# Feed-forward input on un-normed rows: the first two tiles before the norm is known, the row factor applied at their eviction

## The chip, the core and the metric

One core of one Trainium2 chip runs two transformer-like blocks over 512 tokens of width 1024, in float32. The metric is the time of the whole program on the device, in microseconds (us). The engines of the core that appear below are TensorE (PE: matmuls, with PEld for its weight loads), VectorE (DVE), ScalarE (ACT), GpSimd (POOL) and SyncE (SP, which issues the loads of weights). Each runs its own list of instructions in order and waits for the others by semaphores.

## The reference, cut to what matters

```python
def rms_norm(x, g):
    xf = x.astype(jnp.float32)
    xf = xf * lax.rsqrt(jnp.mean(xf * xf, axis=-1, keepdims=True) + RMS_EPS)
    return (xf * g.astype(jnp.float32)).astype(x.dtype)

def modulate(h, shift, scale):
    return h * (1.0 + scale[:, None, :]) + shift[:, None, :]

def swiglu(h, w_in, w_out):
    gate, up = jnp.split(h @ w_in, 2, axis=-1)
    return (jax.nn.silu(gate) * up) @ w_out
...
        h = modulate(rms_norm(x, norm_g[l, 0]), shift[:, 0], scale[:, 0])
        x = x + 0.5 * gate[:, 0, None, :] * swiglu(h, ffn1_w_in[l], ffn1_w_out[l])
        ... token mixer on a second norm ...
        h = modulate(rms_norm(x, norm_g[l, 2]), shift[:, 2], scale[:, 2])
        x = x + 0.5 * gate[:, 2, None, :] * swiglu(h, ffn2_w_in[l], ffn2_w_out[l])
```

With r the factor of a token's row (one number per token), c the combined scale per channel and s the shift per channel, a tile of the feed-forward input is W^T (x c r + s). That equals r times W^T (x c), plus W^T s, which is one number per output channel.

## The kernel before, in words

All activations lie transposed: channels on the 128 partitions, the 512 tokens along the free axis, so a tensor of width 1024 is 8 slabs of 128x512. Each float32 product is made of three passes on parts of reduced width: weights and activations are each split in a high and a low part, and a slab of 128 channels costs three matmuls of 512 columns (high by high, low by high, high by low; lines 431 to 433). The profile calls the activation parts `act_hi` and `act_lo`, the weight parts `w_hi` and `w_lo`.

Weights arrive in chunks of 128x1024, in four rotating buffers. SP loads a chunk into `w_raw` (L426), ACT copies it to the high part (`split_hi`, L382), DVE subtracts to get the low part (`split_lo`, L390), PE uses it for one tile of output in one of four PSUM banks. The splitting runs two chunks ahead of PE (`AHEAD = 2`); where a stage ends, the last splits in its loop belong to the first two chunks of the next stage. The stages follow one another as a list, and on each engine the order is that in which the code is written.

The change touches the two places where a projection back to the residual is followed by a norm and a feed-forward input. The first is `out1`, norm 1, `ffn1_in` (around 700 us), the second `out2`, norm 3, `ffn2_in` (around 1630 us). Each goes as follows:

- `residual` on DVE: for each of the 8 output tiles, split chunk f+2, wait for tile f, add it to the residual slab f. ACT squares the slab (`square`; twice for norm 1, which folds two norms into one and needs two sums), POOL adds the squares of slabs 1 to 6 up.
- `rms_sum` on PE: the squares of all channels are summed per token by matmuls with one column, 8 instructions for norm 3 and 16 for norm 1 (L809). The profile records two entries for each such instruction of plain float32. Then DVE makes a reciprocal, ACT a square root, DVE a diagonal of the factors (`rms_diagonal`), and PE spreads it over the partitions by matmuls with 128 columns into PSUM (L817, for norm 1 also L821).
- `rms` on DVE and `norm_hi` on ACT: for each slab, DVE multiplies residual, scale and factor (L2024), ACT adds the shift and writes `act_hi` (L1535), DVE subtracts to get `act_lo` (L2024). Semaphore `h_ready` counts the slabs.
- `first_pair` on PE: two tiles of the feed-forward input at once, slab by slab as they come, so that six matmuls follow each slab. Then two more tiles, then ten more rounds of four tiles in a loop. In each round, tile 0 and tile 2 are gates (ACT's `Silu`), tile 1 and tile 3 are multiplied with them by DVE, and the product is split into high and low parts for the next stage.

## Time and profile before

| | |
|---|---|
| median of 3 runs | 2020.28 us (2018.68 to 2022.92) |
| the profiled execution's own time | 2020.2 us |
| its span in the trace | 2018.4 us |
| PE busy | 1944.0 us, 96% of the span |
| DVE, ACT, POOL busy | 1000.2, 789.9, 171.1 us |
| mean granted clock of TensorE | 0.984 of full speed |

The span is the time between the first and the last record; the program's own time is 1.8 us longer. Busy times overlap between engines and don't add up to the span. The clock is the share of full speed that was granted to TensorE; it takes two levels, 1.2 and 2.4 GHz, which show as 0.50 and 1.00, and a stretch that holds both shows something between.

### The profile page before, as it was taken

To read this page: it belongs to the slowest core of one execution; us is meant where nothing else is said; L and a number is where in the kernel's file an instruction comes from. 1 tells how busy PE (TensorE), PEld (TensorE's weight loads), DVE (VectorE), ACT (ScalarE), POOL (GpSimd) and SP (SyncE) were. 2 spreads that over 40 slices of the span, in tenths; PEclk is the share of its full clock that TensorE was granted. 3 is DMA by queue.
4 is the path that set the end of the run, shared out by engine and by line. 5 is a ranking of instruction groups with operands and counts; after the bars stand their busy time and mean duration, and the time that the engine had idled before them with its cause. 6 is when DMAs were issued, how large, how long until landed. Compare 5 with 4: busy or idle time off the path is not lost.

```text
span 2018.4 us, 25631 instructions
## 1 busy us (share of the span) xinstructions
PE 1944.0 (96%) x9438; PEld 1590.2 (79%) x9438; DVE 1000.2 (50%) x1434; ACT 789.9 (39%) x1320; POOL 171.1 (8%) x192
## 2 busy tenths in 40 slices
PE   6999999999999999999999899999899999999998
PEld 5888878766788778888887787899688878888886
DVE  5687866575444353333335668454443353333332
ACT  4334333365432344334224644343423244334232
POOL 1101110000000300000001300044000110000000
PEclk9999999999999999999998999999899999999999
DMA  8957913211133322333323223211234323333331
GB/s 291 310 177 233 309 45 97 73 43 38 33 111 118 100 82 88 101 96 93 107 80 110 67 75 90 57 43 53 63 94 130 115 74 94 94 104 91 98 96 50
DMA packets 330629, 212.85 MB, mean 105 GB/s; under 512 B 21358, under 2 KB 315179, under 8 KB 330031
## 3 DMA queue, kind: packets, MB, share of 16 engines
q1 hardware_dynamic: 319024, 170.58, 29.0%
q0 software_dynamic: 10368, 37.75, 5.3%
q10 hardware_dynamic: 1150, 3.35, 0.5%
q8 instruction: 56, 0.92, 0.2%
q14 instruction: 31, 0.25, 0.0%
HBM read 204.31 MB, written 7.35 MB: 105 GB/s over the span
## 4 chain that ended last, share of the span: by engine, by line
PE 84%; DVE 8%; ACT 3%; DMA 2%; issue 2%; ACTq 1%; POOL 0%; DVEq 0%; SPq 0%; POOLq 0%
PE psum L431 24%; PE psum L433 23%; PE psum L432 23%; DVE delta_qkv_T L2024 2%; PE psum L1324 2%; DMA ada_w<-in_ada_w 1%; DVE ada_sum L2024 1%; PE psum L1111 1%; PE psum L1139 1%; DVE w_lo L390 1%; PE psum L1122 1%; PE psum L1007 1%; PE psum L1023 1%; PE psum L1270 1%; DVE act_lo L2024 1%
## 5 line engine op out<-in xcount | busy, mean ns | idle before, releaser
L431 PE MATMUL psum<-act_hi,w_hi 128*128 128x512 f32 x1616 | 648.5, 401 | 8.7 <-DVE act_lo L2024 5.9
L433 PE MATMUL psum<-act_hi,w_lo 128*128 128x512 f32 x1616 | 631.9, 391 | 0.0
L432 PE MATMUL psum<-act_lo,w_hi 128*128 128x512 f32 x1616 | 631.4, 391 | 0.0
L390 DVE TENSOR_TENSOR w_lo<-w_raw,w_hi 128x1024 fp32r<-128x1024 f32 x306 | 382.4, 1252 | 353.2 <-ACT w_hi L382 327.2
L382 ACT ACTIVATE w_hi<-w_raw 128x1024 fp32r<-128x1024 f32 x306 | 319.9, 1053 | 194.3 <-PE psum L433 183.0
L431 PEld LDWEIGHTS psum<-act_hi,w_hi 128*128 128x128 f32 x1616 | 304.9, 189 | 88.5 <-issue 24.1
L433 PEld LDWEIGHTS psum<-act_hi,w_lo 128*128 128x128 f32 x1616 | 304.5, 188 | 65.0
L432 PEld LDWEIGHTS psum<-act_lo,w_hi 128*128 128x128 f32 x1616 | 305.2, 189 | 61.3 <-issue 1.2
L722 POOL TENSOR_TENSOR squares<-squares 128x512 f32<-128x512 f32 x30 | 46.7, 1564 | 1251.1 <-ACT squares L1511 906.9
L431 PE MATMUL psum<-ffn_hi,w_hi 128*128 128x512 f32 x352 | 139.5, 396 | 0.0
L433 PE MATMUL psum<-ffn_hi,w_lo 128*128 128x512 f32 x352 | 139.0, 395 | 0.0
L432 PE MATMUL psum<-ffn_lo,w_hi 128*128 128x512 f32 x352 | 139.0, 395 | 0.0
L1567 ACT ACTIVATE ffn_hi<-ffn_tmp 128x512 f32 x44 | 27.8, 632 | 210.8 <-DVEq L2469 210.8
L2024 DVE SCALAR_TENSOR_TENSOR residual<-psum,params,residual 128x512 f32<-128x512 f32 x24 | 18.0, 751 | 151.4 <-PE psum L433 151.4
L2024 DVE SCALAR_TENSOR_TENSOR ada_sum<-ada_w,params,ada_sum 128x1024 f32<-128x1024 f32 x63 | 80.8, 1282 | 16.8 <-DMA ada_w<-in_ada_w 14.8
L2021 DVE TENSOR_TENSOR ffn_tmp<-ffn_tmp,psum 128x512 f32<-128x512 f32 x44 | 30.2, 687 | 113.4 <-PE psum L433 113.4
L433 PEld LDWEIGHTS psum<-ffn_hi,w_lo 128*128 128x128 f32 x352 | 66.2, 188 | 15.8
L431 PEld LDWEIGHTS psum<-ffn_hi,w_hi 128*128 128x128 f32 x352 | 66.2, 188 | 15.5
L432 PEld LDWEIGHTS psum<-ffn_lo,w_hi 128*128 128x128 f32 x352 | 66.2, 188 | 15.5
L2024 DVE SCALAR_TENSOR_TENSOR delta_qkv_T<-psum,params,delta_qkv_T 128x511 f32<-128x511 f32 (+3 forms) x96 | 60.3, 647 | 35.8 <-ACT delta_qkv_T L1855 33.7
L2021 DVE TENSOR_TENSOR ffn_lo<-ffn_tmp,ffn_hi 128x512 f32 x44 | 30.5, 693 | 46.8 <-ACT ffn_hi L1567 46.8
L431 PE MATMUL psum<-merged_hi,w_hi 128*128 128x512 f32 x128 | 50.6, 395 | 0.0
(343 smaller groups left out, 2331.7 us busy)
## 6 DMA issues: line engine op xcount, KB each, us to landing
w_raw<-in_ffn_w_in SPq DMA_DIRECT2D x88, 512.0 KB, 3.7
ada_w<-in_ada_w POOLq DMA_DIRECT2D x72, 512.0 KB, 5.7
w_raw<-in_w_in SPq DMA_DIRECT2D x68, 512.0 KB, 3.8
w_raw<-in_mix_w_in SPq DMA_DIRECT2D x52, 512.0 KB, 3.7
w_raw<-in_ffn_w_out SPq DMA_DIRECT2D x32, 512.0 KB, 3.8
w_raw<-in_ffn_w_out SPq DMA_DIRECT2D x16, 384.0 KB, 3.3
w_raw<-in_w_branch_a SPq DMA_DIRECT2D x8, 512.0 KB, 3.7
w_raw<-in_w_out SPq DMA_DIRECT2D x8, 512.0 KB, 3.7
```

The source lines that it names most:

```text
L382: act.activation(WHI[:, n % 4, :], RAW[:, n % 4, :], ACT.Copy).then_inc(w_hi, 1)
L390: dve.tensor_tensor(WLO[:, n % 4, :], RAW[:, n % 4, :], WHI[:, n % 4, :].bitcast(F32), ALU.subtract).then_inc(w_lo, 1)
L431: pe.matmul(out, whi, hhi, start=start, stop=False)
L432: pe.matmul(out, whi, hlo, start=False, stop=False)
L433: return pe.matmul(out, wlo, hhi, start=False, stop=stop)
L722: ins = pool.tensor_tensor(SQ[:, q, :], SQ[:, q, :], SQ[:, square_slot(r, k) + q, :], ALU.add)
L1007: mm = pe.matmul(PS[:, 5 + n % 2, 0:T - j * P], QK1[:, 8 + 2 * h + e, j * P:j * P + P], QK1[:, 2 * h + e, j * P:T], start=(e == 0), stop=( ...
L1023: mm = pe.matmul(PS[:, PV_BANK[t % 2], 0:MD + 1], DP[:, h % 2, o:o + P], VTOK[:, j, h, :], start=(j == 0), stop=(j == i))
L1324: mm = pe.matmul(PS[:, bank, (h % 4) * P:(h % 4) * P + P], left(h), right(h), start=True, stop=True)
L1567: act.activation(dst, src, ACT.Copy).then_inc(u_hi, 1)
L2021: return dve.tensor_tensor(o, a, b, op)
L2024: return dve.scalar_tensor_tensor(o, a, s, b, op0, op1)
```

## The change

For `ffn1_in` and `ffn2_in`, the first two tiles are made from the residual times the channel scale, without factor and shift (`raw_pair`). Their activations are written while the projection back still runs: ACT copies each slab with its scale into `act_hi` in `square`, DVE makes `act_lo` in `raw_lo`, one slab later than the residual add. PE runs the two tiles as soon as the projection is done, with the sums of squares, the sums for the shift and the spreading of the factors put in between the slabs. The shift's part, W^T s, is made by DVE from the raw weights of the two chunks (`bias_part`: a product of 128x1024 and a reduction of 1024 to 128 that reads every 128th element) and by two matmuls of one column. The norm then writes the true `act_hi` and `act_lo` over the raw ones, slab by slab, once PE has used them (`raw_used`), and tiles 2 and 3 take the place of the first pair. At eviction DVE multiplies both raw tiles by the factors, ACT applies `Silu` with the shift's sum as bias, and DVE adds the other sum and multiplies. The first round of the loop is written out for this on DVE and ACT, and the factors are copied from PSUM into SBUF by ACT (`RROW`).

```diff
             def rms_sum(r):
...
-                if r == 4:
-                    return
+
+            def rms_spread(r):
+
                 pe.wait_ge(sem("rms_diagonal"), r)
...
+            def raw_pair(r):
+
+                pl = Place(AHEAD_OF[r], 0)
+                banks = [pe_open(pe, pl, t) for t in range(2)]
+                pe.wait_ge(w_lo, pl.chunk + 2)
+                for kk in range(KD):
+                    pe.wait_ge(h_ready, RAW_AT[r] + kk + 1)
+                    for t, bank in enumerate(banks):
+                        n, a = pl.chunk + t, slice(kk * P, kk * P + P)
+                        mm = mm3(pe, bank, WHI[:, n % 4, a], WLO[:, n % 4, a], HHI[:, kk, :], HLO[:, kk, :],
+                                 kk == 0, kk == KD - 1)
+                        if kk == KD - 1:
+                            mm.then_inc(chunk_done, 1)
+                    if kk < KD - 1:
+                        mm.then_inc(sem("raw_used"), 1)
+                    if kk == 1:
+                        rms_sum(r)
+                    elif kk == 2:
+                        pe.wait_ge(sem("bias_parts"), r)
+                        for t in range(2):
+                            mm = pe.matmul(PS[:, 7, t:t + 1], BSUM[:, t, :], ONES[:, 0:1], start=True, stop=True)
+                        mm.then_inc(sem("bias_sum"), 1)
+                    elif kk == 4:
+                        rms_spread(r)
+
+            def after_norm(r):
+
+                raw_pair(r)
+                name = AHEAD_OF[r]
                 pl = Place(name, 0)
-                first_pair([(pl, 0), (pl, 1)], base)
-                for k in range(2, pl.nb):
-                    pe_tile(pe, pl, k, k, KD, HHI, HLO)
+                first_pair([(pl, 2), (pl, 3)], H_AT[r])
...
                 e.then_inc(sem("squares_ready"), 1)
+                if r in RAW_AT:
+                    act.activation(HHI[:, k, :], XT[:, k, :], ACT.Copy, scale=col(COEF_OF[r] + k)).then_inc(sem("h_hi"), 1)
...
+            def before_norm(r):
+
+                pl = Place(AHEAD_OF[r], 0)
+                split_hi(act, pl, 2)
+                root(r)
+                split_hi(act, pl, 3)
+                norm_hi(r, SHIFT_OF[r])
...
+                        if first and f == 0:
+                            act.wait_ge(sem("raw_scaled"), 1 + (name == "ffn2_in"))
+                            act.activation(FS[:, 0, :], FS[:, 0, :], ACT.Silu, bias=col(AG)).then_inc(sem("rows_then_gate"), 1)
...
-                dve.wait_ge(sem("rms_spread"), r)
+                if r in RAW_AT:
+                    split_lo(dve, Place(AHEAD_OF[r], 0), 2)
+                    split_lo(dve, Place(AHEAD_OF[r], 0), 3)
+                    dve.wait_ge(sem("bias_sum"), r // 2 + 1)
+                    dve.tensor_copy(col(AG, 2), PS[:, 7, 0:2]).then_inc(sem("bias_parts"), 1)
+                if r in RAW_AT:
+                    dve.wait_ge(sem("rows_then_gate"), 2 * (r // 2) + 1)
+                    rows = RROW[:]
...
+            def raw_lo(r, k):
+
+                dve.wait_ge(sem("h_hi"), RAW_AT[r] + k + 1)
+                stt(HLO[:, k, :], XT[:, k, :], col(COEF_OF[r] + k), HHI[:, k, :].bitcast(F32), ALU.mult, ALU.subtract)\
+                    .then_inc(h_ready, 1)
+
+            def bias_part(r, t):
+
+                n = Place(AHEAD_OF[r], 0).chunk + t
+                dve.wait_ge(w_loaded[n % 4], 16 * (n // 4 + 1))
+                chained(tt(BPART[:].rearrange("p (k n) -> p k n", n=P), RAW[:, n % 4, :].rearrange("p (k n) -> p k n", n=P),
+                           b3(col(SHIFT_OF[r], KD), P), ALU.mult))
+                ins = dve.tensor_reduce(BSUM[:, t, :], BPART[:].rearrange("p (k n) -> p n k", n=P), AX, ALU.add)
+                chained(ins) if t == 0 else ins.then_inc(sem("bias_parts"), 1)
+
+            def residual(name, per_tile, gate_col, normed=False, r=None):
 
                 pl = Place(name, 0)
                 for f in range(KD):
+                    if r and f:
+                        raw_lo(r, f - 1)
+                    if r and f in (6, 7):
+                        bias_part(r, f - 6)
...
+                        if first and f == 0:
+                            tiles_ready(dve, pl, 1)
+                            cnt.mark(tt(FS[:, 0, :], RROW[:], PS[:, pl.bank(0), :], ALU.mult))
+                            chained(tt(UTMP[:], RROW[:], PS[:, pl.bank(1), :], ALU.mult))
+                            dve.sem_inc(sem("raw_scaled"), 1)
+                            for t in range(2):
+                                dve.sem_inc(bank_free[pl.bank(t)], 1)
+                            dve.wait_ge(sem("rows_then_gate"), 2 + 2 * (name == "ffn2_in"))
+                            chained(stt(FS[:, 0, :], UTMP[:], col(AG + 1), FS[:, 0, :], ALU.add, ALU.mult))
```

The order of instructions on DVE at the end of `out1`, before the change, from the fifth add to the residual on (`residual<-psum,residual` is the add, `w_lo<-w_raw,w_hi` a split; the last two splits are those of the first two chunks of `ffn1_in`):

```order
L2021 TENSOR_TENSOR residual<-psum,residual 128x512
L390 TENSOR_TENSOR w_lo<-w_raw,w_hi 128x1024
L2021 TENSOR_TENSOR residual<-psum,residual 128x512
L390 TENSOR_TENSOR w_lo<-w_raw,w_hi 128x1024
L2021 TENSOR_TENSOR residual<-psum,residual 128x512
```

The same piece after the change, from the sixth add on (`act_lo<-residual,...` is `raw_lo`, `bias_parts` and `bias_sums` are `bias_part`; what each waits for stands behind it):

```order
L2071 TENSOR_TENSOR residual<-psum,residual 128x512 [waits chunk_done]
L2074 SCALAR_TENSOR_TENSOR act_lo<-residual,params,act_hi 128x512 [waits dve_step,h_hi]
L2071 TENSOR_TENSOR bias_parts<-w_raw,params 128x1024 [waits w_loaded3]
L2514 TENSOR_REDUCE bias_sums<-bias_parts 128x128 [waits dve_step]
L392 TENSOR_TENSOR w_lo<-w_raw,w_hi 128x1024 [waits w_hi_ready,dve_step]
L2071 TENSOR_TENSOR residual<-psum,residual 128x512 [waits chunk_done]
L2074 SCALAR_TENSOR_TENSOR act_lo<-residual,params,act_hi 128x512 [waits dve_step,h_hi]
L2071 TENSOR_TENSOR bias_parts<-w_raw,params 128x1024 [waits w_loaded0]
L2514 TENSOR_REDUCE bias_sums<-bias_parts 128x128 [waits dve_step]
L392 TENSOR_TENSOR w_lo<-w_raw,w_hi 128x1024 [waits w_hi_ready]
L2071 TENSOR_TENSOR residual<-psum,residual 128x512 [waits chunk_done]
```

Between two adds there stood one split; now there stand a subtraction that waits for ACT, a product, a reduction and then the split. The last split is that of the second chunk of `ffn1_in`.

On DVE after norm 1, from the last two low parts of the norm to the split of the first chunk of the second round, after the change:

```order
L2074 SCALAR_TENSOR_TENSOR act_lo<-squares,params,act_hi 128x512 x2
L2071 TENSOR_TENSOR ffn_tmp<-rms_rows,psum 128x512
L2071 TENSOR_TENSOR raw_tile<-rms_rows,psum 128x512
L2074 SCALAR_TENSOR_TENSOR ffn_tmp<-raw_tile,params,ffn_tmp 128x512
L2071 TENSOR_TENSOR ffn_lo<-ffn_tmp,ffn_hi 128x512
L392 TENSOR_TENSOR w_lo<-w_raw,w_hi 128x1024 x2
```

The two splits at the end are those of chunks 4 and 5, the first of the second round. They stand behind the whole eviction of the two raw tiles.

## Rows read from the trace of the kernel before

**Rows 1.** The page's chain that ended last, shares of the span by engine

```profile
PE 84%; DVE 8%; ACT 3%; DMA 2%; issue 2%; ACTq 1%; POOL 0%; DVEq 0%; SPq 0%; POOLq 0%
```

**Rows 2.** Timeline of PE, first place: start us, us, engine, line, operation, [idle before <-releaser]

```profile
698.47 1.84 PE L809 MATMUL psum<-constants,squares 128*128 128x1 f32 x16
700.74 3.57 PE L809 MATMUL psum<-constants,squares 128*128 128x1 f32 x16 [0.44 <-ACT squares L1507]
707.43 2.07 PE L817 MATMUL psum<-rms_diagonal,constants 128*128 128x128 f32 x8 [3.12 <-DVE rms_diagonal L2021]
...
711.98 0.47 PE L431 MATMUL psum<-act_hi,w_hi 128*128 128x512 f32 x1 [0.91 <-DVE act_lo L2024]
...
734.60 0.39 PE L431 MATMUL psum<-act_hi,w_hi 128*128 128x512 f32 x1
```

**Rows 3.** Timeline of PE, second place

```profile
1630.95 0.95 PE L809 MATMUL psum<-constants,squares 128*128 128x1 f32 x8
...
1635.24 1.58 PE L817 MATMUL psum<-rms_diagonal,constants 128*128 128x128 f32 x8 [1.51 <-DVE rms_diagonal L2021]
1639.30 0.77 PE L431 MATMUL psum<-act_hi,w_hi 128*128 128x512 f32 x1 [2.47 <-DVE act_lo L2024]
...
1642.76 0.40 PE L433 MATMUL psum<-act_hi,w_lo 128*128 128x512 f32 x1
...
1662.72 0.39 PE L431 MATMUL psum<-act_hi,w_hi 128*128 128x512 f32 x1
```

**Rows 4.** Timeline of DVE: sixth and seventh add of the first place, seventh of the second

```profile
687.47 0.69 DVE L2021 TENSOR_TENSOR residual<-psum,residual 128x512 f32<-128x512 f32 x1 [3.44 <-PE psum L433]
...
693.07 0.69 DVE L2021 TENSOR_TENSOR residual<-psum,residual 128x512 f32<-128x512 f32 x1 [3.44 <-PE psum L433]
...
1625.56 0.75 DVE L2024 SCALAR_TENSOR_TENSOR residual<-psum,params,residual 128x512 f32<-128x512 f32 x1 [3.38 <-PE psum L433]
```

**Rows 5.** Timeline of ACT: squares of the seventh slab, first place; sixth slab, second place

```profile
693.85 0.63 ACT L1506 ACTIVATE squares<-residual 128x512 f32<-128x512 f32 x1 [3.40 <-DVEq L2456]
...
694.39 0.71 ACT L1507 ACTIVATE squares<-residual,params 128x512 f32<-128x512 f32 x1
...
1620.80 0.63 ACT L1511 ACTIVATE squares<-residual 128x512 f32<-128x512 f32 x1 [4.01 <-DVEq L2456]
```

**Rows 6.** Groups by line and form: busy us, mean ns of one, idle before

```profile
L2021 DVE TENSOR_TENSOR cmp_scores<-cmp_scores,params 128x1024 f32<-128x1024 f32 x2 | 2.5, 1225 | 0.1
L2322 DVE TENSOR_REDUCE params<-cmp_scores 128x32 f32<-128x1024 f32 x1 | 1.2, 1220 | 0.0
L2021 DVE TENSOR_TENSOR cmp_blocks<-nsa_kv_T,params 64x248 f32<-64x248 f32 x16 | 8.5, 571 | 0.2
...
L1420 ACT ACTIVATE residual<-residual,params 128x512 f32<-128x512 f32 x8 | 5.8, 724 | 0.3
```

**Rows 7.** The page's costliest groups

```profile
L390 DVE TENSOR_TENSOR w_lo<-w_raw,w_hi 128x1024 fp32r<-128x1024 f32 x306 | 382.4, 1252 | 353.2 <-ACT w_hi L382 327.2
L382 ACT ACTIVATE w_hi<-w_raw 128x1024 fp32r<-128x1024 f32 x306 | 319.9, 1053 | 194.3 <-PE psum L433 183.0
...
L1567 ACT ACTIVATE ffn_hi<-ffn_tmp 128x512 f32 x44 | 27.8, 632 | 210.8 <-DVEq L2469 210.8
```

**Rows 8.** Timeline of DVE, norm 1: its first and its last instructions

```profile
709.54 1.41 DVE L2024 SCALAR_TENSOR_TENSOR squares<-residual,params,psum 128x512 f32<-128x512 f32 x2 [2.17 <-PE psum L817]
...
719.01 1.63 DVE L2024 SCALAR_TENSOR_TENSOR act_lo<-squares,params,act_hi 128x512 fp32r<-128x512 f32 x2
```

**Rows 9.** Stretches: busy us (x records) PE, PEld, DVE, ACT, POOL; granted clock; DMA, GB/s

```profile
700.00:702.00 2.00, 1.56 (x9) 1.48 (x9) 0.34 (x2) 1.98 (x3) 0.00 (x0) 0.64 0.00 0
...
80.00:82.00 2.00, 2.00 (x19) 2.00 (x20) 0.00 (x0) 1.91 (x4) 0.53 (x1) 1.00 1.02 327
...
230.00:232.00 2.00, 2.00 (x11) 2.00 (x10) 1.50 (x2) 1.43 (x2) 0.53 (x1) 0.50 0.84 279
```

**Rows 10.** Timeline of PE, early in the program: sums of one column after a gap

```profile
227.64 1.95 PE L834 MATMUL psum<-constants,ada_sum 128*128 128x1 f32 x16 [1.48 <-DVE ada_sum L2024]
```

More of the change, by code:

```diff
@@ L2487, in _ @@
             chained(tt(col(FCOEF, 8), col(COEF, 8), col(FNG, 8), ALU.mult))
-            rms(1, FCOEF, idx=1, shift=MOD)
+            residual("out1", 1, None, r=1)
+            rms(1, FCOEF, MOD)
             ffn_in("ffn1_in")
```

104 lines of the change are left out of this document (60 added, 44 removed).

## The prediction

> **What bounds the kernel now.** I read the chain of waits first. PE holds 84% of it [rows 1], so a change counts by what it takes from or adds to PE's own line. Then I read PE's timeline at the two places. At the first, PE has its last matmul of `out1` behind it at 698.47 us and starts the first of `ffn1_in` at 711.98: 13.51 us, in which it does the sums of squares in two halves (1.84 us, then 3.57 for the same number), waits 3.12 for DVE's diagonal and spreads the factors [rows 2]. At the second the same stretch runs from 1630.95 to 1639.30, 8.35 us [rows 3]. The round behind the first four tiles starts at 734.60 and at 1662.72 [rows 2, 3]. These two marks are where before and after are to be compared, because the work up to them is the same four tiles and the rounds behind them are untouched. For the sum I also need the lists of DVE and ACT while the projection still runs. There DVE sits idle 3.4 us ahead of each add [rows 4], and ACT squares as soon as the add is done [rows 5]. PE passes a tile there in 5.60 us (687.47 to 693.07).
>
> A matmul of 512 columns follows the one before by 0.227 us: 88 in the 19.96 us from 1642.76 to 1662.72 [rows 3]. At the low clock it is about 0.43: eight took 3.46 us, from 1639.30 to 1642.76, the first ones at half speed, where 1.81 would do [rows 3]. A half sum (8 instructions, 16 records) takes 1.84 us at the high clock and 3.57 at the low one [rows 2].
>
> **What the change adds ahead of PE.** Price of the detour on DVE between two adds, taken from the sixth add at the first place. The add starts at 687.47 and takes 0.69 [rows 4]; ACT starts 0.09 later and squares twice, 1.25 us (693.85 to 695.10 on the next slab) [rows 5]; then the new copy, 0.72 as the copy with a scale of the same form [rows 6]; then DVE's subtraction, 0.75 as a L2024 of this size (the add of the second place, [rows 4]); the product with the shift, 1.23, and the reduction, 1.22 [rows 6]; the split 1.25 [rows 7]. With some 0.2 of hand-over and overlap on balance the seventh add starts at 695.0, not at 693.07. The second detour starts from there and has the same terms, only that the split stands behind it and PE waits for it: 695.0 + 0.69 + 0.09 + 1.25 + 0.72 + 0.75 + 1.23 + 0.2 + 1.22 + 1.2 gives 702.2 for the second chunk's low part. PE needs it at 698.47. So the raw pair **starts with a stall of 3.7 us**. At the second place there is one square (0.63) and the add takes 0.75: 1619.96 (the start of the sixth add, one tile of 5.60 ahead of 1625.56 [rows 4]) leads to 1626.9 and then to 1633.5, against 1630.95, a stall of 2.6 us. The detour costs nothing up to the fifth slab, where there is only copy and subtraction and the 3.4 us of idle time hold them. That POOL's adding and the second sum come later too has no price: they are ready before PE is through the first two slabs.
>
> The reduction is the one price with two sides. By operation and size the nearest row is 1.22 us for 1024 elements, read in order. But this one reads every 128th. The nearest row that reads with a step is the product on 248 elements at 0.571 us, where 0.4 would follow from 1.225 for 1024 and 0.69 for 512 [rows 4, 6], so up to 0.63 ns more per element, and 1.86 us for 1024. I take 1.22, the row of the operation itself, and keep 1.86 for the range. The Trainium skill speaks against the change here: "SBUF — State Buffer", in the part on Door 1, the DMA port swizzle, says that each access that goes on to a new 16-byte line pays a penalty, which every element of this reduction would do. By that rule the upper figure is the right one, and the sum is 2.6 us higher than by the row of the operation.
>
> **What it costs on PE at the high clock.** First place, from 702.2: two slabs of the raw pair 2.7, both half sums 3.7, one slab 1.4, two bias sums 0.5 (four records of 0.115), two slabs 2.7, two spreads of 8 records 1.8 (0.115 each: 1.84 for 16 records of one column, and the spread of the second place, 1.58, has part of itself at the low clock [rows 3]), three slabs 4.1, the true pair 10.9. Its end is at 730.0. DVE needs the diagonal 3.1 us behind the sums; slabs and bias sums hide that. So the wait of 3.12 goes.
>
> What is late next is the far end. The first spread ends at 714.1. ACT copies the rows (0.6), and DVE's norm takes 11.1 us (709.54 to 720.64, [rows 8]), to 725.9. Only then come the eviction and the splits that stand behind it: two scalings 1.4, `Silu` 0.6, the add and product 0.75, the copy to `ffn_hi` 0.63, the split of chunk 4 on ACT 1.05 and on DVE 1.25 [rows 7], with 0.7 of hand-overs 6.4 us, to **732.3**. PE waits there from 730.0, 2.3 us. Against 734.60 the first place gains 2.3. Second place, from 1633.5, with one half sum and one spread: the spread ends at 1643.6, DVE's side at 1661.8, and PE, done at 1658.6, waits 3.2. Against 1662.72 it gains 0.9. So with a high clock throughout the sum is −3.2 us.
>
> **What the clock does to it.** In the trace of before the clock fell at the first place some 2 us after the last dense matmul: the second half of the sums ran at low speed, and the stretch from 700 to 702 holds 0.64 [rows 2, 9]. It rose only after the spreads. Early in the program a gap of 1.48 us and 1.95 us of sums of one column were enough: the stretch behind them shows 0.50 [rows 9, 10]. The new stalls of 3.7 and 2.6 us with nothing at all are as long. So I expect the low clock at the start of the raw pair, and at the first place again after the 3.7 us of sums with one column. First place: twelve matmuls at low speed, +2.4; one of two half sums, +1.7; about two thirds of the eighteen matmuls between the sums and the spread, +2.7; in all +6.8, all of it ahead of the spread, and so not hidden by the wait at the far end. Second place: one such stretch as the trace has it there, +1.7 (3.46 less 1.81). Bounds: nothing, and both blocks low up to the spread, about +12 and +9.
>
> The sum: first place −2.3 + 6.8 = +4.5, second place −0.9 + 1.7 = +0.8, together **+5.3 us**. The profiled execution took 2020.2, against a median of 2020.28, so the forecast is **2025.5 us**. All else I cost at nothing: the bias product moves no load, since the buffers are freed by the same split, 1.9 and 3.6 us later, while the next chunks are needed more than 10 us on; the table loads that leave the loops were on ACT, which has idle time in every round.
>
> **The rivals.**
>
> Clock stays up. If 2.6 and 3.7 us of waiting between dense stretches do not lower it, there is the gain of 3.2 us: 2017.0. For it speaks that at 80 to 82 us 1.95 us of sums between dense matmuls left it at 1.00 [rows 9]. Against it speak both stretches named above. The page "TensorE: Matmul & The Clock Gate" of the Trainium skill, under "HAM oscillation", says that short waits for data between groups of matmuls bring the low clock back each time; by it the low stretches come. Chance 0.15. It decides at the opening stall: under 1.5 us this would be the case.
>
> Slow reduction. With 1.86 instead of 1.22, four reductions add 2.6 us, two to each opening stall: 2028.1. Chance 0.17.
>
> Detour hidden. If DVE's detour ended ahead of the need for the second chunk (product and reduction together in 0.6 us instead of 2.45, which takes 1.85 from each detour and 3.7 from two), both stalls would go, and the low clock of the opening with them: −3.2 − 3.7 − 2.6 = −9.5, 2010.7. Only the 3.4 us of idle time [rows 4] speak for it; the wait for ACT's copy in the middle speaks against it. Chance 0.05.
>
> Forecast, with its own range of 2021.5 to 2031, chance 0.63.
>
> **How the numbers follow.** A measurement of this kernel can tell about 0.2% from no change, that is 4.0 us: 2016.2 to 2024.3. The range of 8 in 10 leaves out the hidden detour and the far end of the low clock, and takes in the high clock's 2017.0: 2017.0 to 2032.0. Faster: the hidden detour and a quarter of the first rival, 0.09. Same: the rest of that rival and the lower part of the forecast, 0.26. Slower: the rest, 0.65.
>
> **What the profile after would show.** The raw pair's first matmul with an idle time of 3 to 4 us at the first place and 2 to 3 at the second, released by DVE's `w_lo`; a reduction of 1.2 or 1.9 us; a clock of 0.50 in the first slabs; no wait of PE for `rms_diagonal`; a second wait for `w_lo`, 2 to 3 us, ahead of the second round. The second round's start less the end of the projection was 36.13 and 31.77 us before; I expect 40.6 and 32.6. It would be wrong if PE starts the raw pair without waiting, or if the stretches named show 1.00.

## The result, and the profile after

The changed kernel takes 2031.01 us (median of 5 runs, 2029.08 to 2037.39), beside it the kernel before 2018.68 us. The ratio is 1.0069, with a 95% interval of 1.0042 to 1.0095: **slower by 12.3 us**, where 5.3 was forecast. The time lies inside the predicted range of 8 in 10 (2017.0 to 2032.0) and 0.01 us above the forecast's own (2021.5 to 2031). Sign and place are as predicted, the size is more than twice the forecast.

The profiled execution took 2037.39 us (span 2035.7, mean granted clock 0.981), the longest of the five and 17.2 us more than that of before. These 17.2 us are found again on PE's own timeline. The projection of the first place ends 3.2 us later than before (701.70 against 698.47; another execution of the changed kernel had it at 696.55, so this part is scatter of the earlier program). From the end of the projection to the second round it was 36.13 and 31.77 us; now it is 46.13 and 34.07. Another 1.6 us is low clock behind the second place. 10.0 + 2.3 + 1.6 is 13.9, and with the 3.2 it is 17.1.

The timeline of PE, to be laid beside [rows 2, 3] (start us, us, engine, line, operation, idle before and its releaser):

```profile
701.47 0.40 PE L435 MATMUL psum<-merged_hi,w_lo 128*128 128x512 f32 x1
...
713.11 0.77 PE L433 MATMUL psum<-act_hi,w_hi 128*128 128x512 f32 x1 [11.25 <-DVE w_lo L392]
...
747.83 0.50 PE L433 MATMUL psum<-act_hi,w_hi 128*128 128x512 f32 x1 [1.80 <-DVE w_lo L392]
...
1643.84 0.40 PE L435 MATMUL psum<-merged_hi,w_lo 128*128 128x512 f32 x1
1648.63 0.55 PE L433 MATMUL psum<-act_hi,w_hi 128*128 128x512 f32 x1 [4.39 <-DVE w_lo L392]
...
1678.14 0.50 PE L433 MATMUL psum<-act_hi,w_hi 128*128 128x512 f32 x1 [2.69 <-DVE w_lo L392]
```

The projection ends one matmul (0.23 us) behind the first and the fourth row. Four waits of PE, all for a low part of weights that DVE hasn't split yet, hold 20.1 us. The two in front of the raw pair are the opening stalls, the two in front of the second round the far-end stalls. No wait for `rms_diagonal` is left at the two places; that part of the change does what it says.

The list of PE's waits, after (us in total, times, longest):

```profile
PE psum L433 <- DVE w_lo L392: 20.1, 4, 11.2
```

What DVE does while PE waits stands in its timeline. Two tiles before the first detour, and both detours:

```profile
688.19 0.68 DVE L2071 TENSOR_TENSOR residual<-psum,residual 128x512 f32<-128x512 f32 x1
690.85 1.27 DVE L2074 SCALAR_TENSOR_TENSOR act_lo<-residual,params,act_hi 128x512 fp32r<-128x512 f32 x1 [1.99 <-ACT act_hi L1542]
692.05 2.31 DVE L392 TENSOR_TENSOR w_lo<-w_raw,w_hi 128x1024 fp32r<-128x1024 f32 x1
694.28 0.68 DVE L2071 TENSOR_TENSOR residual<-psum,residual 128x512 f32<-128x512 f32 x1
696.95 1.27 DVE L2074 SCALAR_TENSOR_TENSOR act_lo<-residual,params,act_hi 128x512 fp32r<-128x512 f32 x1 [1.99 <-ACT act_hi L1542]
698.14 2.31 DVE L2071 TENSOR_TENSOR bias_parts<-w_raw,params 128x1024 f32<-128x1024 f32 x1
700.49 1.95 DVE L2514 TENSOR_REDUCE bias_sums<-bias_parts 128x128 f32<-128x1024 f32 x1
702.47 1.23 DVE L392 TENSOR_TENSOR w_lo<-w_raw,w_hi 128x1024 fp32r<-128x1024 f32 x1
703.62 0.68 DVE L2071 TENSOR_TENSOR residual<-psum,residual 128x512 f32<-128x512 f32 x1
...
711.55 1.22 DVE L392 TENSOR_TENSOR w_lo<-w_raw,w_hi 128x1024 fp32r<-128x1024 f32 x1
```

Three numbers there weren't in the prediction. `act_lo` takes 1.27 us, not 0.75. The split and the product take 2.31 us where the same split took 1.23 at 702.47. And the adds, which stood 5.60 us apart before [rows 4], stand 6.09 apart already at 688.19 and 694.28, ahead of any shift sum, and DVE's idle time ahead of them, 3.44 us before, is gone: DVE is slower per tile than PE and falls behind. What makes them slow can't be seen in DVE's own list. It is in POOL's:

```profile
690.28 2.99 POOL L726 TENSOR_TENSOR squares<-squares 128x512 f32<-128x512 f32 x2 [3.10 <-ACT squares L1535]
696.37 3.00 POOL L726 TENSOR_TENSOR squares<-squares 128x512 f32<-128x512 f32 x2 [3.10 <-ACT squares L1535]
```

The slow `act_lo`, splits and products of DVE are those that run beside POOL's adds, the quick splits (702.47, 711.55) stand where POOL is idle. The two reductions, at 700.49 and 709.76, stand where POOL is idle too. The reduction, by tile name (ns, min, median, max), took the upper price of the prediction's two:

```profile
L2514 DVE TENSOR_REDUCE bias_sums<-bias_parts x4: 1871/1911/1998, 700.5 to 1645.4; 128x128 f32<-128x1024 f32 x4
```

Granted clock in stretches of the first place (us, busy us and records of PE, PEld, DVE, ACT, POOL; PEclk; DMA share; GB/s): the stall, the two slabs, the sums, the slabs behind them, the rest:

```profile
701.70:713.10 11.40, 0.17 (x1) 0.02 (x1) 9.35 (x8) 1.85 (x3) 2.94 (x2) 0.72 0.16 46
713.10:717.80 4.70, 4.69 (x13) 3.71 (x14) 1.02 (x2) 4.08 (x5) 0.00 (x0) 0.58 0.38 112
717.80:722.00 4.20, 4.20 (x33) 4.20 (x32) 0.00 (x0) 0.00 (x0) 0.00 (x0) 0.82 0.00 0
722.00:727.00 5.00, 5.00 (x15) 4.13 (x16) 4.37 (x10) 1.26 (x2) 0.00 (x0) 0.50 0.00 2
727.00:747.80 20.80, 19.04 (x92) 15.68 (x90) 15.02 (x23) 11.20 (x15) 0.00 (x0) 0.99 0.17 51
```

### The profile page after: what moved, and what is told of

It is laid out like the page before. It is cut to its first block, busy times and chain, and to the rows that moved or that the text cites. A ratio compares the mean times of both kernels' runs of the same rounds, so it can differ in the third digit from the quotient of the medians.

```text
span 2035.7 us, 25625 instructions
## 1 busy us (share of the span) xinstructions
PE 1951.1 (96%) x9446; PEld 1594.0 (78%) x9446; DVE 1037.6 (51%) x1464; ACT 744.6 (37%) x1296; POOL 170.6 (8%) x192
## 4 chain that ended last, share of the span: by engine, by line
PE 82%; DVE 10%; ACT 3%; issue 2%; DMA 2%; ACTq 1%; POOL 0%; DVEq 0%; SPq 0%; POOLq 0%
PE psum L433 23%; PE psum L434 22%; PE psum L435 22%; DVE delta_qkv_T L2074 2%; DVE w_lo L392 2%; PE psum L1353 2%; DMA ada_w<-in_ada_w 1%; PE psum L1140 1%; DVE ada_sum L2074 1%; DVE act_lo L2074 1%; PE psum L1168 1%; PE psum L1151 1%; PE psum L1036 1%; PE psum L1052 1%; PE psum L1299 1%
## 5 line engine op out<-in xcount | busy, mean ns | idle before, releaser
L433 PE MATMUL psum<-act_hi,w_hi 128*128 128x512 f32 x1616 | 652.4, 404 | 24.9 <-DVE w_lo L392 20.1
L392 DVE TENSOR_TENSOR w_lo<-w_raw,w_hi 128x1024 fp32r<-128x1024 f32 x306 | 386.5, 1266 | 335.5 <-ACT w_hi L384 314.2
L1612 ACT ACTIVATE ffn_hi<-ffn_tmp 128x512 f32 (+1 forms) x44 | 27.8, 632 | 206.8 <-DVEq L2562 206.8
L1877 ACT ACTIVATE ffn_tmp<-psum 128x512 f32<-128x512 f32 x42 | 25.2, 599 | 109.6 <-PE psum L435 109.6
L2071 DVE TENSOR_TENSOR ffn_lo<-ffn_tmp,ffn_hi 128x512 f32 (+1 forms) x44 | 30.5, 692 | 50.0 <-ACT ffn_hi L1612 50.0
```

Of the source, the lines that this page charges most:

```text
L392: dve.tensor_tensor(WLO[:, n % 4, :], RAW[:, n % 4, :], WHI[:, n % 4, :].bitcast(F32), ALU.subtract).then_inc(w_lo, 1)
L433: pe.matmul(out, whi, hhi, start=start, stop=False)
L1612: act.activation(dst, src, ACT.Copy).then_inc(u_hi, 1)
L1877: act.activation(FS[:, f, :], PS[:, pl.bank(2 * f), :], ACT.Silu)\
L2071: return dve.tensor_tensor(o, a, b, op)
```

## The experiments

Twelve kernels ran, in three groups on one chip each, every one beside the kernel before: e1 to e4; `after_again`, e5, e7 and e8; e6 and e10 to e12. Beside its first measurement, the changed kernel ran only in the second group, so across groups the ratios are the sounder comparison. "Mark" is the time from the projection's end to the second round's first matmul; "low" counts the 512-column matmuls between the raw pair's start and the second round that follow each other by about 0.43 us instead of 0.227, and what they cost more, both places together. Marks, stalls and low counts are of the profiled execution.

| kernel | opening stalls, us | marks, us | low | median, us | ratio to before (95%) |
|---|---|---|---|---|---|
| before | | 36.13, 31.77 | 7, 1.5 us | 2018.6 to 2019.4 | |
| after (the result) | 11.41, 4.56 | 46.13, 34.07 | 27, 5.8 us | 2031.01 | 1.0069 (1.0042 to 1.0095) |
| after_again | 11.10, 4.55 | 46.01, 35.35 | 33, 7.2 us | 2034.85 | 1.0076 (1.0059 to 1.0094) |
| e1_no_pool_adds | 4.70, 3.50 | 39.58, 33.04 | 27, 5.8 us | 2023.06 | 1.0012 (0.9997 to 1.0027) |
| e2_no_shift_sums | 5.01, 0 | 39.47, 27.84 | 19, 4.0 us | 2021.73 | 1.0017 (1.0000 to 1.0034) |
| e3_reduce_in_order | 10.11, 3.13 | 44.05, 32.65 | 27, 5.5 us | 2028.49 | 1.0046 (1.0029 to 1.0062) |
| e4_splits_first | 0, 0 | 32.81, 29.26 | 10, 2.3 us | 2014.49 | 0.9975 (0.9961 to 0.9989) |
| e5_splits_first_far_end | 0, 0 | 30.87, 26.40 | 9, 2.1 us | 2007.93 | 0.9945 (0.9926 to 0.9964) |
| e6_far_end | 11.33, 4.55 | 42.98, 31.23 | 24, 5.1 us | 2025.48 | 1.0041 (1.0028 to 1.0054) |
| e7_pool_after_lo | 0, 0 | 29.28, 26.40 | 6, 1.3 us | 2009.25 | 0.9944 (0.9926 to 0.9962) |
| e8_sums_apart | 0, 0 | 27.95, 26.37 | 0 | 2004.39 | 0.9925 (0.9910 to 0.9939) |
| e10_shift_sums_later | 0, 0 | 27.97, 25.10 | 0 | 2002.43 | 0.9921 (0.9909 to 0.9933) |
| e11_no_adds_no_shift | 0, 0 | 32.83, 27.85 | 8, 1.9 us | 2013.91 | 0.9975 (0.9964 to 0.9986) |
| e12_no_adds_in_order | 3.28, 2.09 | 37.22, 30.03 | 19, 4.0 us | 2019.89 | 1.0008 (0.9995 to 1.0021) |

(The stalls of this table run from the end of the last matmul, counted as 0.23 us; the bracket in the profile is 0.16 or 0.17 smaller. In e8 and e10 PE also waits 0.25 us ahead of the second round of the first place, at a clock of 1.00.)

### after_again: the changed kernel beside the others

> The changed kernel itself, beside the others on one chip, so that their differences from it can be taken. 2031 us within 2, ratio to the kernel before 1.005 to 1.008; the opening stalls of 11.2 and 4.4 us and the far-end stalls of 1.8 and 2.7 us come again to 0.1 us.

No edit. The ratio is 1.0076, as expected; the median is 3.8 us above the first one, and the first opening stall came again to 0.3 us, not to 0.1, the other three stalls to 0.01. What differs between the two executions is the low clock: 33 low matmuls here, 27 in the first profile. The stalls are a property of the program, the count of low matmuls up to the second round is partly chance, by some 1.5 us.

### e1: POOL's adding left out

```diff
                 for k in range(1, KD - 1):
                     pool.wait_ge(sem("squares_ready"), NT + 8 * (r - 1) + k + 1)
+                    if r in RAW_AT:
+                        pool.sem_inc(sem("squares_added"), 1)
+                        continue
```

> Leaves out POOL's adding of the squares of slabs 1 to 6 at both places (the norm factor is made from two slabs). Theory A (POOL and DVE slow each other when POOL adds squares while DVE makes act_lo and splits or multiplies): act_lo goes from 1.27 to 0.75 us and the 2.31 us splits and products to 1.23, DVE keeps up with PE's 5.6 us a tile, the opening stall falls from 11.25 to 4 to 5 us at the first place and from 4.39 to 3.5 to 4 at the second, and the program takes 5 to 8 us less than the changed kernel: 2023 to 2026. Theory B (POOL is no cause; the detour is long by the reductions and by waiting for ACT alone): act_lo stays at 1.27, the stalls stay within 1 us, and the time stays at 2031 within 2 us.

Theory A held: `act_lo` has a mean of 752 ns, the splits 1223 and the products 1220, the first opening stall falls to 4.7 us. The groups of DVE between 600 and 720 us, first of the changed kernel (repeated run), then of e1 (busy us, mean ns):

```profile
L392 DVE TENSOR_TENSOR w_lo<-w_raw,w_hi 128x1024 fp32r<-128x1024 f32 x21 | 30.0, 1431 | 12.2 <-ACT w_hi L384 11.5
L2074 DVE SCALAR_TENSOR_TENSOR act_lo<-residual,params,act_hi 128x512 fp32r<-128x512 f32 x8 | 9.1, 1142 | 15.9 <-ACT act_hi L1542 15.9
...
L2071 DVE TENSOR_TENSOR bias_parts<-w_raw,params 128x1024 f32<-128x1024 f32 x2 | 4.6, 2296 | 0.0
```

```profile
L392 DVE TENSOR_TENSOR w_lo<-w_raw,w_hi 128x1024 fp32r<-128x1024 f32 x22 | 26.9, 1223 | 12.4 <-ACT w_hi L384 11.6
L2077 DVE SCALAR_TENSOR_TENSOR act_lo<-residual,params,act_hi 128x512 fp32r<-128x512 f32 x8 | 6.0, 752 | 15.9 <-ACT act_hi L1545 15.9
...
L2074 DVE TENSOR_TENSOR bias_parts<-w_raw,params 128x1024 f32<-128x1024 f32 x2 | 2.4, 1220 | 0.0
```

The collision costs 6.7 us of stall at the first place (6.4 against the repeated run), where POOL adds twice per slab, and 1.1 at the second, where it adds once.

### e2: the shift sums left out

```diff
-                n = Place(AHEAD_OF[r], 0).chunk + t
-                dve.wait_ge(w_loaded[n % 4], 16 * (n // 4 + 1))
-                chained(tt(BPART..., RAW..., b3(col(SHIFT_OF[r], KD), P), ALU.mult))
-                ins = dve.tensor_reduce(BSUM[:, t, :], ..., AX, ALU.add)
+                ins = dve.memset(BSUM[:, t, :], 0.0)
```

> Leaves out the product and the reduction for the shift's part in the first two tiles (a fill with zeros of 128 elements takes their place). Theory A (DVE is full over the whole projection by contention, and the detours only come on top): 6 us of the first place's opening stall go (two products of 2.3 and 1.2 and two reductions of 1.9, less what they hid), so 4 to 5 us of the 11.25 remain there; at the second place the 4.39 us go to under 1; time 8 to 10 us less than the changed kernel, 2021 to 2023. Theory B (the detours alone make the stalls): both opening stalls go under 1 us and with them the low clock behind them, time 12 to 16 us less, 2015 to 2019.

Theory A's numbers, 5.0 us left at the first place and nothing at the second. So at the first place the raw pair would start late even if the detours cost nothing: DVE is already behind when the projection ends. At the second place, with one add per slab, there is no stall without the detours; the collision makes it longer once they are there.

### e3: the reduction reads in order

```diff
-                ins = dve.tensor_reduce(BSUM[:, t, :], BPART[:].rearrange("p (k n) -> p n k", n=P), AX, ALU.add)
+                ins = dve.tensor_reduce(BSUM[:, t, :], BPART[:].rearrange("p (n k) -> p n k", k=KD), AX, ALU.add)
```

> Computes wrong sums for the shift: the reduction adds eight neighbours instead of eight elements 128 apart, with the same number of elements read and written. If the step of the reading is what makes it 1.87 to 2.0 us, it falls to 1.22, each opening stall loses 1.3 to 1.6 us, and the time falls by 2.5 to 4 us, to 2027 to 2028.5. If the reduction is long by its form or by POOL's adding beside it, it stays at 1.87 and the time at 2031.

```profile
L2514 DVE TENSOR_REDUCE bias_sums<-bias_parts x4: 1220/1220/1220, 698.0 to 1639.9; 128x128 f32<-128x1024 f32 x4
```

The same instruction on the same number of elements takes 1220 ns in order and 1871 to 1998 with a step of 128 elements. POOL's adds aren't the reason: in e1, without them, the four reductions still take 1.87 to 1.99 us. The stalls fall by 1.3 and 1.4 us (1.0 and 1.4 against the repeated run). That is the prediction's second rival in cause, and in the size of the stalls (2.7 us together, where it gave 2.6). The times can't fix the size: they give 2.5 us against the first median of the changed kernel, 4.6 by the ratios, 6.1 by the ratio of the repeated run.

### e11: both left out

The edits of e1 and e2 together.

> Leaves out both POOL's adding of squares and DVE's product and reduction for the shift. Alone, the one left a first opening stall of 4.5 us and the other 4.8, of 11.3. If the two causes share one slack (DVE's idle time of a tile), both out leaves no stall, and neither is the remainder of a third cause: opening stalls under 0.5 us at both places, time 2012 to 2016, as in e4. If a third thing (waiting for ACT's copy, the split's place behind it) holds the raw pair up, 1 us or more is left.

No stall is left in front of either raw pair, and the time is e4's. With the adds alone out 4.7 us of the 11.4 were left, with the shift sums alone out 5.0; 6.7 and 6.4 together are more than there is, so the two causes use up the same idle time. No third cause stands behind them; ACT's copy in the middle of each tile (DVE waits 1.99 us for it) is harmless once DVE has the room.

### e12: the changed kernel at the prediction's prices

The edits of e1 and e3 together. DVE's prices are then the very ones of the prediction's sum.

> Leaves out POOL's adding of squares and computes wrong shift sums by reading in order: DVE's prices are then those that the prediction used, 0.75 for act_lo, 1.23 for split and product, 1.22 for the reduction. If its model was right but for the two prices, the opening stalls are its 3.7 and 2.6 us (by e1's 4.5 and 3.3 less 1.3 to 1.4 for the reductions, rather 3.2 and 2.0), the marks from the projection's end to the second round its 40.6 and 32.6, within 1.5, and the time 2019 to 2023. If the model itself was wrong, the marks are off by more than 2 us.

DVE's timeline through both detours:

```profile
685.35 0.69 DVE L2074 TENSOR_TENSOR residual<-psum,residual 128x512 f32<-128x512 f32 x1 [1.04 <-PE psum L435]
688.02 0.75 DVE L2077 SCALAR_TENSOR_TENSOR act_lo<-residual,params,act_hi 128x512 fp32r<-128x512 f32 x1 [1.98 <-ACT act_hi L1545]
688.69 1.22 DVE L2074 TENSOR_TENSOR bias_parts<-w_raw,params 128x1024 f32<-128x1024 f32 x1
689.94 1.22 DVE L2517 TENSOR_REDUCE bias_sums<-bias_parts 128x128 f32<-128x1024 f32 x1
691.19 1.22 DVE L392 TENSOR_TENSOR w_lo<-w_raw,w_hi 128x1024 fp32r<-128x1024 f32 x1
692.34 0.68 DVE L2074 TENSOR_TENSOR residual<-psum,residual 128x512 f32<-128x512 f32 x1
...
699.20 0.68 DVE L2074 TENSOR_TENSOR residual<-psum,residual 128x512 f32<-128x512 f32 x1
```

From the sixth add to the end of the last split, where the eighth add starts, it is 13.9 us; the prediction had 687.47 to 702.2, 14.7. PE starts 0.4 us behind it, and the stalls are 3.28 and 2.09, where it had 3.7 and 2.6. But the marks are 37.22 and 30.03, and it had 40.6 and 32.6: this was the last outcome of the expectation, off by more than 2 us. Most of this is the low clock, priced at 6.8 and 1.7 us, where 19 low matmuls cost 4.0 us at the first place and none was low at the second. The stretches behind the two stalls of e12, first that of 3.28 us, then that of 2.09 (the clock is the number behind POOL's):

```profile
699.60:704.90 5.30, 5.27 (x13) 4.19 (x14) 1.03 (x2) 4.09 (x5) 0.00 (x0) 0.50 0.33 99
1630.60:1633.50 2.90, 2.90 (x14) 2.40 (x14) 1.15 (x2) 2.39 (x4) 0.00 (x0) 1.00 0.58 170
```

### e4: the weight splits first

```diff
+                    for c in range(per_tile):
+                        split_lo(dve, pl, per_tile * f + c + AHEAD)
                     if r and f:
                         raw_lo(r, f - 1)
-                    if r and f in (6, 7):
-                        bias_part(r, f - 6)
-                    for c in range(per_tile):
-                        split_lo(dve, pl, per_tile * f + c + AHEAD)
+                    if r and f == 7:
+                        bias_part(r, 0, 0)
...
                 if r:
+                    bias_part(r, 0, 1)
                     raw_lo(r, KD - 1)
+                    bias_part(r, 1)
```

The third argument 0 stands for the product alone, 1 for the reduction alone. SP's loads for the second round now wait until the shift sums have read the raw weights. Nothing is left out.

> The whole computation, with DVE's order changed: in each tile the weight split before raw_lo, the product for chunk 0 ahead of the last add, the reduction for chunk 0 behind it, raw_lo of the last slab then, product and reduction for chunk 1 last, so that PE waits for no shift sum before it starts the raw pair. If the order on DVE is what the opening stall consists of, both opening stalls fall under 2 us, with the low clock behind them; the bias sums are then waited for inside the raw pair, for at most 1 to 2 us. First place's mark 46.1 goes to 36 to 39, second's 34.1 to 31 to 32.5, time 2018 to 2023. If DVE is behind by contention whatever the order, the stall of the first place only moves into the pair (waits for act_lo or for bias_parts of 4 us and more) and the time stays above 2026.

PE goes from the projection into the raw pair without a gap, at both places:

```profile
701.56 0.39 PE L435 MATMUL psum<-merged_hi,w_lo 128*128 128x512 f32 x1
701.79 0.39 PE L433 MATMUL psum<-act_hi,w_hi 128*128 128x512 f32 x1
...
734.60 0.50 PE L433 MATMUL psum<-act_hi,w_hi 128*128 128x512 f32 x1 [1.75 <-DVE w_lo L392]
```

The shift sums are waited for once, 1.13 us inside the second raw pair. 2014.49 us is below all that was expected, and 0.25% below the kernel before: the same instructions in another order take 16.5 us less than the changed kernel's first median, 19 us by the ratios. In this order the split runs ahead of POOL's adds and keeps its 1.23 us; `act_lo` still meets them, and one product does (2.31 us at 700.53), in time that DVE has to spare.

### e5 and e6: the far end

```diff
                         if first and f == 0:
+                            split_hi(act, pl, 4)
                             act.wait_ge(sem("raw_scaled"), ...)
...
                             for t in range(2):
                                 dve.sem_inc(bank_free[pl.bank(t)], 1)
+                            split_lo(dve, pl, 4)
                             dve.wait_ge(sem("rows_then_gate"), ...)
...
-                            split_lo(dve, pl, 2 * f + AHEAD)
+                            if not first:
+                                split_lo(dve, pl, 2 * f + AHEAD)
```

e5 is e4 with this edit, e6 the changed kernel with it.

> The whole computation: the order of e4_splits_first, and at the far end both parts of chunk 4 split ahead of the gate (ACT before the scalings are done, DVE right behind them). If the stall ahead of the second round (1.75 and 2.68 us in e4) is the weight split standing behind the gate's chain, both waits go, and the low clock behind the second one (about 1.7 us) with them: 4 to 6 us less than e4's 2014.5, 2008.5 to 2010.5. If the round waits for the banks or for the gate's product instead, the wait stays over 1 us at both places under another name and the time is within 1.5 us of e4's.

> The changed kernel with the far end's edit alone: both parts of chunk 4 split ahead of the gate, all else as it was. If the far-end stall is the weight split behind the gate's chain, and its price is the same whatever the opening does, the waits of 1.80 and 2.69 us ahead of the second round go and the low clock behind the second one with them: 4 to 6 us less than the changed kernel's 2031 to 2035, the opening stalls stay at 11.2 and 4.4. If the far end only hides part of what the opening loses, it gives under 2 us.

Both far-end stalls are gone in both. In e5 the second round follows without a gap (730.49 and 730.72 on PE), and the time is 6.6 us below e4's (6.1 by the ratios). In e6 the opening stalls stay at 11.33 and 4.55 and the marks fall by 3.0 to 3.2 and 2.8 to 4.1 us; what goes beyond the stalls of 1.95 and 2.85 us is fewer low matmuls, 24 against 27 and 33. The far-end stall was within 0.05 us of 1.95 and 2.85 in every kernel without this edit, whatever stood in front of it. Its two sides, DVE's norm and PE's last slabs, both start at the spread, so nothing ahead of the spread changes it, and nothing hides it. DVE in e6, at the first place, has the split of chunk 4 between the scaling and the gate's product:

```profile
738.35 0.68 DVE L2073 TENSOR_TENSOR raw_tile<-rms_rows,psum 128x512 f32<-128x512 f32 x1
739.37 1.23 DVE L392 TENSOR_TENSOR w_lo<-w_raw,w_hi 128x1024 fp32r<-128x1024 f32 x1 [0.34 <-DVE raw_tile L2073]
740.51 0.74 DVE L2076 SCALAR_TENSOR_TENSOR ffn_tmp<-raw_tile,params,ffn_tmp 128x512 f32<-128x512 f32 x1
```

### e7: POOL's adds behind `act_lo`

```diff
                     if k > 1:
                         pool.wait_ge(sem("squares_added"), 6 * (r - 1) + k - 1)
+                    if r in RAW_AT:
+                        pool.wait_ge(h_ready, RAW_AT[r] + k + 1)
```

On top of e5, with nothing left out.

> The whole computation: as e5_splits_first_far_end, but POOL adds the squares of a slab only after DVE's act_lo of that slab. No work is left out, only the overlap of POOL's add with act_lo goes. If the two take turns on something shared, the one behind waiting until the one ahead is done, act_lo falls from 1.27 us (first place) and 1.79 (second) to 0.75 in every slab but those beside the product, POOL's two adds from 3.0 to 2.55 and its single one from 1.8 to 1.3, and the wait for the shift sums inside the second raw pair (1.13 us in e4) goes or halves; time within 1.5 us of e5's, because PE hardly waits for it. If act_lo is long by itself, it stays at 1.27 and 1.79.

One slab of e7, DVE and then POOL:

```profile
682.39 0.75 DVE L2083 SCALAR_TENSOR_TENSOR act_lo<-residual,params,act_hi 128x512 fp32r<-128x512 f32 x1 [0.51 <-ACT act_hi L1549]
685.31 0.69 DVE L2080 TENSOR_TENSOR residual<-psum,residual 128x512 f32<-128x512 f32 x1 [2.17 <-PE psum L435]
```

```profile
683.31 2.55 POOL L733 TENSOR_TENSOR squares<-squares 128x512 f32<-128x512 f32 x2 [3.03 <-DVE act_lo L2083]
```

With every addition still made, `act_lo` has a mean of 751 and 748 ns at the two places (1178 and 1530 in e5) and POOL's two adds take 2.55 us. So it is the overlap that costs, not the amount of work. The add on the residual, which begins at 685.31 while POOL adds until 685.86, isn't slower for it; it has one operand in PSUM, while `act_lo`, split and product read both from SBUF. The time is e5's, as expected, since the collision had moved to where DVE has room. What the delay of POOL's adds alone would do to the changed kernel's stalls was not run. One part was a miss: the wait of 1.13 us for the shift sums stayed to the hundredth. They start from the last add and wait for nothing of POOL's.

### e8 and e10: the sums of squares apart, the shift sums later

```diff
-                    if kk == 1:
-                        rms_sum(r)
-                    elif kk == 2:
+                    late = int(r == DOUBLE)
+                    if kk == 1:
+                        rms_sum(r, (0,) if late else (0, 1))
+                    elif kk == 2 and late:
+                        rms_sum(r, (1,))
+                    elif kk == 2 + late:
                         pe.wait_ge(sem("bias_parts"), r)
...
-                    elif kk == 4:
+                    elif kk == 4 + late:
                         rms_spread(r)
```

Both on top of e5; e10 has `elif kk == 3:` in place of `elif kk == 2 + late:`, and is e8 otherwise.

> The whole computation: as e5_splits_first_far_end, but at the first place PE does the second half of the sums of squares one slab later than the first, the shift sums and the spreading one slab later too. At the second place 1.7 us of one-column matmuls left the clock at 1.00, at the first 3.9 us in one piece brought 0.50 for some 11 matmuls. If the length of one stretch of thin work decides, the low clock behind the sums goes at the first place, 2 to 3 us less than e5. If it is the amount of thin work in both stretches together, the low clock comes all the same, one slab later, and the time stays within 1 us of e5's or rises by 1, since the spread, and with it the norm, come a slab later.

> The whole computation: e8_sums_apart with PE's shift sums one slab later at the second place too, where they were waited for 1.13 us. The wait goes (a slab is 1.36 us), and the time is about 1 us less than e8's 2004.4, 2003 to 2004.5, which the measurement can hardly tell; what tells is the wait in the trace. If it only turned up again in front of the spread or of the second round, the mark there would stay the same to 0.3 us.

PE's clock over the sums and behind them, first in e5 (sums in one piece, then the slabs), then in e10 (first half and a slab, second half and a slab, the rest):

```profile
702.60:707.00 4.40, 4.40 (x33) 4.40 (x32) 4.33 (x4) 3.21 (x4) 0.00 (x0) 0.78 0.00 0
707.00:712.00 5.00, 5.00 (x15) 4.13 (x16) 4.55 (x11) 1.26 (x2) 0.00 (x0) 0.51 0.53 156
```

```profile
702.00:705.50 3.50, 3.50 (x25) 3.15 (x23) 3.19 (x4) 2.52 (x4) 0.00 (x0) 1.00 0.00 0
705.50:708.80 3.30, 3.30 (x25) 3.04 (x24) 3.27 (x3) 1.57 (x2) 0.00 (x0) 1.00 0.00 0
708.80:715.00 6.20, 6.20 (x38) 5.43 (x38) 4.76 (x12) 1.76 (x3) 0.00 (x0) 1.00 0.70 195
```

The same 32 records of one-column matmuls, with PE busy throughout, are followed by the low clock in one piece and leave it at 1.00 in two pieces with six dense matmuls between them. The mark of the first place falls by 2.9 us and the time by 3.5. In e10 the wait for the shift sums is gone and the second mark falls by 1.27 us more. At 2002.43 us **e10 beats both kernels**: 0.79% below the one before, with the interval 0.9909 to 0.9933, and 28.6 us below the changed one's first median (30 by the ratios), with the same arithmetic.

## Why the prediction came out too small

**The mechanism was there, but it doesn't make the measured time.** The diagonal's wait is gone. The raw pair waits for DVE's split of the second chunk, released by `w_lo`; the clock is low behind it; a second wait for `w_lo` stands in front of the second round. All of these are in the trace where the prediction had them. At the prediction's prices they come to no slowdown: e12 has a ratio of 1.0008 (0.9995 to 1.0021). What makes the changed kernel slower is what the prediction put at nothing, the collision with POOL, and the reduction, which it took at the lower of its two prices.

**"The detour costs nothing up to the fifth slab", and "That POOL's adding and the second sum come later too has no price".** These two steps failed, and they are the largest miss: DVE had no idle time left up to the fifth slab, and POOL's adding cost 6.7 us of the first opening stall. Before, POOL's adds began 1.16 us behind the start of the split, just as that ended. DVE and POOL in the trace of before, one tile of the first place:

```profile
671.61 1.22 DVE L390 TENSOR_TENSOR w_lo<-w_raw,w_hi 128x1024 fp32r<-128x1024 f32 x1 [0.25 <-DVE residual L2021]
...
672.77 2.54 POOL L722 TENSOR_TENSOR squares<-squares 128x512 f32<-128x512 f32 x2 [3.06 <-ACT squares L1507]
```

Now ACT's second square sends POOL to its adds (690.28), and ACT's copy sends DVE to `act_lo` 0.57 us later (690.85), while the first add runs. DVE's `act_lo` waits until POOL's first add is done (1.27 instead of 0.75), and what follows it, split or product, until the second is (2.31 instead of 1.22). POOL pays too: its two adds take 3.00 us instead of 2.54. Each tile costs 1.6 us more, the 3.4 us of idle time don't hold that beside the wait for ACT, and DVE runs at 6.09 us a tile against PE's 5.60. That, with the slower reduction, is why the first opening stall is 11.4 us and not 3.7. e1 puts the collision's share at 6.7 us, and e7 shows that the overlap, not the work, makes `act_lo` long. The Trainium skill has this rule in "SBUF — State Buffer", "Who interferes with whom": a DVE instruction with two SBUF inputs and a GpSimd instruction that reads SBUF share a read port, whichever starts first keeps it for its whole length, and the other waits. The traces agree: waiting times of 0.5 and 1.1 us behind adds of 1.29, and no slowing of the add that has one operand in PSUM. The prediction drew on this page for another rule and didn't weigh this one.

The price stood in the trace of before, at other places. Five splits between 1913 and 1977 us began some 0.4 us behind the start of an add of POOL and took 2.32 or 2.33 us; six between 986 and 1064 began at 1.2 us behind one and took 1.55. The first of the five, POOL and DVE:

```profile
1913.44 1.67 POOL L722 TENSOR_TENSOR squares<-squares 128x512 f32<-128x512 f32 x1 [284.51 <-ACT squares L1511]
...
1913.87 2.32 DVE L390 TENSOR_TENSOR w_lo<-w_raw,w_hi 128x1024 fp32r<-128x1024 f32 x1
```

What no row could show is that the change brings DVE's new instructions to the same moment as POOL's adds. For that, POOL's line had to be laid over DVE's new list, as was done with ACT's.

**"I take 1.22, the row of the operation itself".** The reduction was mis-sized. It measured 1.87 to 2.00 us, at or above the upper bound of 1.86 that was worked out from the 248-element product. The rule in the Trainium skill, "SBUF — State Buffer", in the part on Door 1, that each access on a new 16-byte line pays a penalty, named the right one of the two. The trace agrees, and e3 shows that the step is the cause: 1.22 us in order. Two reductions to a stall make 1.3 and 1.4 us of it.

**"First place: ... in all +6.8 ... Second place: ... +1.7".** The clock was priced too high for the stalls that were forecast: e12, with nearly those stalls, shows +4.0 and nothing. At the first place the half sum that was to run at low speed, +1.7, ran at the high one (32 records in 3.84 us, 3.7 expected), and 19 matmuls were low where the sum had 24. For the twelve of them between the sums and the spread it took 2.7, where the first twelve were priced at 2.4. With the longer real stalls it was 4.2 and 1.6 (4.6 and 2.5 in the repeated run), and 1.6 to 4.5 us more behind the far-end stalls, which the sum didn't contain. The rival of the high clock was wrong at the first place in every run with a stall there, and right at the second only for the 2.09 us of e12. What the prediction quoted against it, that short waits bring the low clock back each time, held for the stalls of 3.13 us and more, but not each time below that.

**The far end.** "PE waits there from 730.0, 2.3 us" and "3.2" measured 1.95 and 2.85 (1.91 to 1.96 and 2.84 to 2.85 in eight executions). The term was a little too large because the hand-overs overlap more than was taken: in e12 the steps from the first scaling to the end of the split take 5.9 us (727.62 to 733.51), not 6.4.

The balance: at the prediction's prices (e12) the marks are 37.22 and 30.03, together 0.65 us less than before, where the sum had +5.3: the clock, the stalls and the far end were together about 6 us too high. On top come 8.9 us at the first and 4.0 at the second place for the collision and the step in the reduction, with the low clock that followed the longer stalls, and 1.6 us of low clock behind the second place. So two errors of opposite sign met in the forecast of 5.3: a clock priced too high, and a collision and a reduction priced too low. That the sign agrees is luck.

## What to carry to other kernels

When work on one engine is moved, lay the new list of every engine that shares memory ports with it over the old ones, moment by moment: an instruction that now starts together with another engine's can cost its neighbour's whole length. The price may stand in the trace of before, at a place where the two already meet, as it did here; that they will meet at the new place doesn't. A wait for an engine's result is set by what stands ahead of it in that engine's list: the same instructions with the split that PE waits for put first went from 2031 to 2014 us, and to 2008 with the same done at the far end. Thin work on PE can be cheaper in pieces between dense matmuls than in one: 3.5 us here, e5 against e8.

## What was not expected of the hardware

- DVE and POOL take turns rather than share. At the second place of e5 the split began at 1620.57 and kept its 1.23 us while POOL's add, begun at 1621.13, took 1.82 instead of 1.29; `act_lo`, behind it at 1621.71, took 1.79 instead of 0.75, until 0.55 us after POOL's end at 1622.95. In both pairs the one that started first ran on and the other waited.
- An opening stall of 2.09 us left the clock at 1.00 (e12, second place, one execution); stalls of 3.13 us and more were followed by a stretch at 0.50 at all twelve places that had one.
- What follows a far-end stall isn't the same from run to run. Behind that of 2.85 us there is no low matmul in e1, e3 and e12, 6 to 8 in e2, e4, e11 and the first profile of the changed kernel, 14 in the second. Behind that of 1.95 us there were 8, in the second profile of the changed kernel alone. What decides between them stays open.
